# Step sizes by token, sums by triangular matmuls, and a reordered hand-over between two stages of a hybrid block kernel

## The reference, cut to what matters

```python
proj = h @ even_w_in                 # z 512, xbc 1024, dt 8, u 512 columns
z, xbc, dt = split(zxbcdt)
xbc = silu(causal_depthwise_conv(xbc, conv_w, conv_b)); xs, bm, cm = split(xbc)
dt = softplus(dt + dt_bias)          # 512 tokens x 8 heads
a_cs = cumsum(dt * -exp(a_log))      # along the tokens
y = (cm @ bm^T * exp(a_cs[l] - a_cs[s]), causal) @ (xs * dt) + d_skip * xs
y_a = rmsnorm_by_group(y * silu(z)) * norm_gain
y_b = s5_mixer(u)                    # complex-diagonal state space, then a GLU (w_glu)
x = x + concat(y_a, y_b) @ even_w_out
```

## Time and profile before

| | us |
|---|---|
| median of 3 runs | 2755.56 |
| lowest, highest | 2754.64, 2760.26 |
| the profiled execution, device time | 2758.86 |
| its span, first to last instruction | 2757.1 |
| granted TensorE clock, share of full | 0.997 |

### The profile page before, as it was taken

The page is one execution under the profiler, slowest core; times in us unless marked ns, Lnnn a source line. Parts: engine busy times, 40 slices in busy tenths (PEclk is TensorE's granted clock), DMA queues, the critical chain, the costliest instruction groups (busy, mean ns, idle before and its releaser), DMA issues. The chain is left out here.

```text
span 2757.1 us, 33783 instructions
## 1 busy us (share of the span) xinstructions
PE 2704.5 (98%) x12890; PEld 2210.6 (80%) x12890; DVE 1415.8 (51%) x1813; ACT 965.0 (35%) x1350; POOL 223.2 (8%) x212
## 2 busy tenths in 40 slices
PE   8999999899999999999999999999999999999998
PEld 7888877778888888888877888888888787788887
DVE  6676247654443344443486544333898635633334
ACT  5433223543332233332245333222323642422312
POOL 2000014020000000000221000000000000300003
PEclk9999999999999999999999999999999999999999
DMA  4334235232223222232321223333442024222331
GB/s 160 122 134 170 97 116 148 68 122 94 97 99 107 91 89 94 99 107 98 113 69 54 97 93 99 113 107 111 141 135 84 32 70 136 77 99 97 105 105 52
DMA packets 78513, 282.74 MB, mean 103 GB/s; under 512 B 10304, under 2 KB 11456, under 8 KB 77648
## 3 DMA queue, kind: packets, MB, share of 16 engines
q1 hardware_dynamic: 67952, 249.67, 27.2%
q0 software_dynamic: 5856, 25.47, 2.8%
q10 hardware_dynamic: 4608, 6.30, 0.9%
HBM read 261.21 MB, written 13.89 MB: 100 GB/s over the span
## 5 line engine op out<-in xcount | busy, mean ns | idle before, releaser
L201 DVE TENSOR_TENSOR wl<-raw,wh 128x1024 fp32r<-128x1024 f32 (+2 forms) x439 | 564.9, 1287 | 1067.3 <-ACT wh L195 1065.5
L195 ACT ACTIVATE wh<-raw 128x1024 fp32r<-128x1024 f32 (+2 forms) x440 | 480.6, 1092 | 1106.9 <-PE PS L249 919.4
L247 PE MATMUL PS<-Hh,wl 128*128 128x512 f32 x2160 | 846.4, 392 | 9.3 <-DVE wl L201 6.1
L249 PE MATMUL PS<-Hl,wh 128*128 128x512 f32 x2160 | 840.7, 389 | 0.0
L248 PE MATMUL PS<-Hh,wh 128*128 128x512 f32 x2160 | 840.6, 389 | 0.0
L247 PEld LDWEIGHTS PS<-Hh,wl 128*128 128x128 f32 x2160 | 405.5, 188 | 101.0 <-issue 14.9
L248 PEld LDWEIGHTS PS<-Hh,wh 128*128 128x128 f32 x2160 | 405.6, 188 | 85.0 <-issue 1.9
L249 PEld LDWEIGHTS PS<-Hl,wh 128*128 128x128 f32 x2160 | 405.5, 188 | 84.6
L247 PE MATMUL PS<-ffn_gh,wl 128*128 128x512 f32 x880 | 342.7, 389 | 0.0
L249 PE MATMUL PS<-ffn_gl,wh 128*128 128x512 f32 x880 | 342.3, 389 | 0.0
L248 PE MATMUL PS<-ffn_gh,wh 128*128 128x512 f32 x880 | 342.3, 389 | 0.0
(11 more groups left out here) (492 smaller groups left out, 2563.6 us busy)
## 6 DMA issues: line engine op xcount, KB each, us to landing
raw<-in_gu SPq DMA_DIRECT2D x220, 512.0 KB, 3.6
raw<-in_dn SPq DMA_DIRECT2D x80, 704.0 KB, 4.0
raw<-in_hin SPq DMA_DIRECT2D x44, 512.0 KB, 3.6
raw<-in_oin SPq DMA_DIRECT2D x16, 512.0 KB, 3.7
raw<-in_hin_gate SPq DMA_DIRECT2D x16, 512.0 KB, 3.6
X<-QKV ACTq DMA_DIRECT2D x96, 64.0 KB, 2.0
kept_x<-X POOLq DMA_DIRECT2D x16, 256.0 KB, 3.8
raw<-in_eout SPq DMA_DIRECT2D x8, 512.0 KB, 4.0
```

Of the source, the lines that this page charges most:

```text
L195: self.nc.scalar.activation(self.wh[j % SPLIT][:, 0:kw], self.raw[j][:, 0:kw], ACT.Copy).then_inc(self.hi_ready, 1)
L201: self.nc.vector.tensor_sub(self.wl[j % SPLIT][:, 0:kw], self.raw[j][:, 0:kw], self.wh[j % SPLIT][:, 0:kw].bitcast(F32)).then_inc(self.lo_ ...
L247: self.nc.tensor.matmul(out, wl, xh[:, u.k0 + k, :], start=first, stop=False)
L249: done = self.nc.tensor.matmul(out, wh, xl[:, u.k0 + k, :], start=False, stop=last)
```

## The change

- dt becomes part of the u units: a `SideUnit` has ten chunks, eight into its own bank and two into bank 6. The dt stage of four small units is gone.
- `take` scales 8 x 512 once; four matmuls (`turn`) put it by token into 128 x 32, and every later step works on 128 x 32 tiles. The scan gives way to ten matmuls of eight columns with a triangle and ones (`running_sums`). `finish` moves from the second bc unit to the first.
- TOE has a buffer of its own, zeroed by POOL at the start of `even_input` and filled there by POOL's DMAs. `sh_seg` moves into the buffer of Hl.
- The last z unit's read and SiLU, the second split of the GLU weights and the second masking of `CB` move from the end of `even_input` to the start of the joint stage. The 12 products of ones become 2, and 3 and 8 more stand in the first quarter of the joint stage.
- The first two units of the output projection run chunks 4 to 7 in one go each; DVE makes parts 0 and 1 and splits both units ahead of the gates; ACT splits the second unit ahead of a gate.
- `SPLIT_STEP` goes from 6 to 16.
- The table `cols` grows from 310 to 324 columns and the filler `skew` shrinks from 40 to 25, so table and filler together are 349 columns rather than 350.

```diff
 TT = S // P
-SPLIT_STEP = 6
+SPLIT_STEP = 16
+TABLES = 349
...
+class SideUnit(Unit):
+    def __init__(self, kc, side, src, x, bank, side_k0, side_bank, side_start, side_stop):
+        super().__init__(kc + side, src, x, 0, bank)
+        self.main, self.side_k0, self.side_bank = kc, side_k0, side_bank
+        self.side_start, self.side_stop = side_start, side_stop
+    def at(self, k):
+        if k < self.main:
+            return self.bank, k, k == 0, k == self.main - 1
+        return (self.side_bank, self.side_k0 + k - self.main, self.side_start and k == self.main,
+                self.side_stop and k == self.kc - 1)
...
         self.M8 = self.sb("M8", [P, S5G])
-        self.skew = self.sb("skew", [P, 40])
+        self.skew = self.sb("skew", [P, TABLES - dram["cols"].shape[1]])
...
-        v, c0 = self.co.nc.vector, self.co.cols
-        x, e, q, z, z2, rl = self.rows
+        co = self.co
+        self.step(dve, co.nc.vector.tensor_mul(self.ROW, co.PS[0:SSD_H, DT_BANK, :], co.RS[0:SSD_H, :]))
+    def turn(self, pe):
+        co = self.co
+        pe.wait_ge(self.ready, 1)
...
+                                    co.ident[0:SSD_H, 0:SSD_H], start=True, stop=True)
+        m.then_inc(self.turned, 1)
+    def begin(self, dve):
+        v = self.co.nc.vector
+        x, e, q, z, z2, rl, a = self.rows
         k = self.cols["dt_bias"]
-        self.step(dve, v.tensor_mul(x, self.co.PS[0:SSD_H, 4, :], self.co.RS[0:SSD_H, :]))
-        self.step(dve, v.tensor_scalar(x, x, c0[0:SSD_H, k:k + 1], None, ALU.add))
+        bias = self.co.cols[:, k:k + SSD_H].unsqueeze(1).broadcast_to([P, TT, SSD_H])
+        dve.wait_ge(self.turned, 1)
+        self.step(dve, v.tensor_add(self.by_head(x), self.by_head(self.co.PS[:, 7, 0:TT * SSD_H]), bias))
...
         a, k = self.co.nc.scalar, self.cols["a_log"]
-        a.activation(self.W[:, 6, 0:1], self.co.cols[0:SSD_H, k:k + 1], ACT.Exp).then_inc(self.exped, 1)
...
         a.activation(self.rows[1], self.rows[1], ACT.Exp, scale=-1.0).then_inc(self.exped, 1)
+        a.activation(self.A8, self.co.cols[:, k:k + SSD_H], ACT.Exp).then_inc(self.exped, 1)
...
+        x, e, q, z, z2, rl, a = self.rows
...
-        g.memset(self.AT, 0.0).then_inc(self.filled, 1)
...
         v = self.co.nc.vector
-        x, e, q, z, z2, rl = self.rows
+        x, e, q, z, z2, rl, a = self.rows
+        dt = self.AC[:, 32:64]
         dve.wait_ge(self.pooled, 15)
-        self.step(dve, v.scalar_tensor_tensor(self.DT[:], q, 2.0, rl, ALU.mult, ALU.add))
-        self.step(dve, v.tensor_scalar(x, self.DT[:], self.W[:, 6, 0:1], -1.0, ALU.mult, ALU.mult))
-        dve.wait_ge(self.filled, 2)
-        self.step(dve, v.tensor_tensor_scan(self.AT[0:SSD_H, :], self.co.ones8[:], x, 0.0, ALU.mult, ALU.add))
+        dve.wait_ge(self.exped, 2)
+        self.step(dve, v.scalar_tensor_tensor(dt, q, 2.0, rl, ALU.mult, ALU.add))
+        self.step(dve, v.scalar_tensor_tensor(self.by_head(a), self.by_head(dt), -1.0,
+                                              self.A8.unsqueeze(1).broadcast_to([P, TT, SSD_H]), ALU.mult, ALU.mult))
+    def running_sums(self, pe):
+        co, a = self.co, self.rows[6]
+        pe.wait_ge(self.ready, SIZE_STEPS)
+        for t in range(TT):
+            out = co.PS[:, 7, 32 + t * SSD_H:32 + (t + 1) * SSD_H]
+            for k in range(t + 1):
+                m = co.nc.tensor.matmul(out, co.triu if k == t else co.ones[:], a[:, k * SSD_H:(k + 1) * SSD_H],
+                                        start=k == 0, stop=k == t)
+        return m
...
 XBUF = 2
-SIZE_STEPS = 11
+SIZE_STEPS = 10
+DT_BANK = 6
+FILL = (2, 3, 8)
+def cut_products(co, CB, g):
+    d = CB[:, g, 0:S].rearrange("p (t n) -> p t n", n=P)
+    return co.nc.vector.tensor_mul(d, d, co.triu.unsqueeze(1).broadcast_to([P, TT, P]))
...
+    toe_zeroed, toe_in = co.soft_sem("toe_zeroed"), co.soft_sem("toe_in")
+    table = co.dram["s5_k"].rearrange("(m i) n -> i m n", i=16)
...
             def columns():
-                pe.wait_ge(sizes.ready, SIZE_STEPS)
-                for k, src in enumerate((AT[0:SSD_H, :], DT)):
-                    for t in range(TT):
-                        m = nc.tensor.matmul(co.PS[:, 7, (k * TT + t) * 8:(k * TT + t + 1) * 8], src[:, t * P:(t + 1) * P],
-                                             co.ident[0:8, 0:8], start=True, stop=True)
-                m.then_inc(cols_done, 1)
+                sizes.running_sums(pe).then_inc(cols_done, 1)
...
+            def after_x(n):
+                if n == 0:
+                    sizes.turn(pe)
...
             co.multiply(pe, st_u, bank_free)
-            co.multiply(pe, st_dt, dt_bank_free)
-            co.multiply(pe, st_x, bank_free, after=4)
+            co.multiply(pe, st_x, bank_free, after=4, between=after_x)
...
             co.multiply(pe, st_z, bank_free, after=12, between=after_z)
-            pe.wait_ge(z_taken, 1)
-            co.idle_products(0, 12)
+            co.idle_products(0, FILL[0])
...
             d = co.dram["s5_u"]
+            nc.gpsimd.memset(TOE[:, 0:BL - 1, :], 0.0).then_inc(toe_zeroed, 1)
...
             sizes.series(pool)
+            pool.wait_ge(toe_zeroed, 1)
+            for m in range(BL):
+                pool.dma_start(TOE[16 * m:16 * m + 16, BL - 1 - m:BL, :], table[:, 0:m + 1, :]).then_inc(toe_in, 16)
...
             pool.wait_ge(arrived, 16 * len(loads))
-            co.wait_units(pool, st_z, 0, 3)
-            nc.gpsimd.memset(co.Hl[:, 0:BL - 1, :].bitcast(F32), 0.0).then_inc(co.toe_zeroed, 1)
+            pool.wait_ge(toe_in, 16 * BL)
...
             def read_conv(n):
+                if n == 1:
+                    sizes.exponentials(act)
...
                     silu(7)
+                if c == 3:
+                    return
...
             co.run(act, st_u, co.split_hi, lambda i, c: None)
-            co.run(act, st_dt, co.split_hi, lambda i, c: None)
-            co.run(act, st_x, co.split_hi, lambda i, c: read_conv(c), lambda: sizes.exponentials(act))
+            co.run(act, st_x, co.split_hi, lambda i, c: read_conv(c))
             co.run(act, st_bc, co.split_hi, lambda i, c: read_conv(4 + c))
-            co.run(act, st_z, co.split_hi, read_z)
+            co.run(act, st_z, co.split_hi, read_z, late=True)
...
             v = nc.vector
-            dve.sem_inc(dt_bank_free, 1)
...
                 dve.sem_inc(bank_free, 1)
-            def read_dt(i, c):
-                co.wait_units(dve, st_dt, i, c)
-                sizes.take(dve)
+                if c == 3:
+                    sizes.take(dve)
...
                 dve.sem_inc(bank_free, 1)
+                if n == 0:
+                    sizes.begin(dve)
...
                     taps(n - 1)
-                if n == 5:
+                if n == 1:
+                    sizes.quotient(dve)
+                if n == 4:
...
             def read_z(i, c):
+                if c == 3:
+                    return
...
                     take_tokens(3)
-                if c >= 2:
-                    g = c - 2
-                    dve.wait_ge(cb_read, g * TT + TT)
-                    d = CB[:, g, 0:S].rearrange("p (t n) -> p t n", n=P)
-                    v.tensor_mul(d, d, co.triu.unsqueeze(1).broadcast_to([P, TT, P])).then_inc(cut_off, 1)
+                if c == 2:
+                    dve.wait_ge(cb_read, TT)
+                    cut_products(co, CB, 0).then_inc(cut_off, 1)
             co.run(dve, st_u, co.split_lo, read_u)
-            co.run(dve, st_dt, co.split_lo, read_dt)
-            co.run(dve, st_x, co.split_lo, lambda i, c: read_conv(st_x, c, c), lambda: sizes.quotient(dve))
+            co.run(dve, st_x, co.split_lo, lambda i, c: read_conv(st_x, c, c))
             co.run(dve, st_bc, co.split_lo, lambda i, c: read_conv(st_bc, c, 4 + c))
-            co.run(dve, st_z, co.split_lo, read_z, take_columns)
+            co.run(dve, st_z, co.split_lo, read_z, take_columns, late=True)
...
     with ExitStack() as ctx:
-        SEG = co.sb("sh_seg", [P, 3, TRI], ctx=ctx)
+        SEG = co.sb_at("sh_seg", [P, 3, TRI], F32, co.x_end + 4 * DC * S)
...
         T = lambda q: DRIVE[:, 8 * q + 4:8 * q + 8, :].rearrange("p g n -> p (g n)")
-        toe_in = co.soft_sem("sh_toe_in")
+        z_taken, z_active, cut_off = (co.sem(f"sh_{s}") for s in ("z_taken", "z_active", "cut_off"))
...
         def _(sp):
-            table = d["s5_k"].rearrange("(m i) n -> i m n", i=16)
-            sp.wait_ge(co.toe_zeroed, 1)
-            for m in range(BL):
-                sp.dma_start(TOE[16 * m:16 * m + 16, BL - 1 - m:BL, :], table[:, 0:m + 1, :]).then_inc(toe_in, 16)
...
                              d["s5_out"][:, 1024 * q:1024 * q + 1024]).then_inc(arrived[q], 16)
-            sp.wait_ge(toe_in, 16 * BL)
...
                 if q == 0:
-                    pe.wait_ge(toe_in, 16 * BL)
+                    pe.wait_ge(z_taken, 1)
...
                 spread_a(2 * q)
+                if q == 0:
+                    co.idle_products(7, FILL[1])
...
```

(78 more changed lines are left out.)

49 lines of the change are left out of this document (21 added, 28 removed).

## The result

The changed kernel takes 2761.25 us, median of 14 runs (2760.49 to 2766.52); the kernel before took 2757.31 beside it, median of 14 (2753.79 to 2760.26). The ratio is 1.0017, 95% interval 1.0011 to 1.0024: 4 us slower, clear of zero but within the 0.2% or so that the prediction counts as no change, where 16.6 us less was forecast. The profiled execution has a span of 2759.5 us at a granted clock of 0.999.

The account below looks back on a forecast made before the run. PE, busy 98% of the span, was taken as the bound. Gains of 4.7 + 2.9 + 4.5 + 2.4 + 2.1 = 16.6 us took the profiled 2758.86 to 2742.3; less 3.3 to the median, 2739.0, range 2731 to 2748.

Parts of the forecast that it names:

- Table and filler: Stage buffers behind tables and filler: every one moves by 4 bytes, taken as no gain, 2 us either way.
- input stage, stalls less new matmuls: Even mixer's input stage: PE's stalls on DVE's splits shrink, 6.2 us gained, less 1.5 for new column matmuls: 4.7.
- hand-over: From last z unit to first drives on PE: 4.99 us becomes 2.1, gain 2.9, bounds 2.4 to 3.4.
- joint stage: Drives to DVE's second-quarter read: 23.87 us becomes 19.4 with PE at full clock, gain 4.5, bounds 0.9 to 5.
- output begin: Start of the output projection: two PE stalls of about 1.1 us go, gain 2.4, bounds 1.2 to 2.5.
- attention stages: Banded and window attention: the split moved to step 16 lands where ACT and DVE idle, gain 2.1, bounds 1 to 2.3.
- rival (a): PE at half clock from the hand-over into the second quarter; joint gain 0.9 rather than 4.5: 2742.6 us, chance 0.14.
- rivals (a) to (d): Beyond (a), (b): (c) late DMA loads, 2747, chance 0.08; (d) stalls partly stay, 2741.5, 0.05, or all stay, 2751, 0.04.
- rival (b): Joint stage: clock low through all four quarters, 28 us more, 2771 us, slower than before; chance 0.06.

Follow-up runs that it names:

- 348-column version: The changed kernel with its filler one column shorter, so stage buffers begin at byte 118912 as in the kernel before: 2739.50 us, ratio 0.9941 to the kernel before.

## Why the prediction was wrong

The step that failed is "Table and filler": "Every stage buffer moves by 4 bytes. No row shows a price for a position in either direction; I take nothing and 2 us either way." It is wrong twice. The buffers moved by 32 bytes, since the allocator rounds up. And the 2 us had no row behind it: the kernel before holds its large matmuls at one distance modulo 256, so its trace could not show what another one costs, and the edit touches 3408 matmuls on an engine that is busy for 98% of the span. 2 us was 0.6 ns a matmul; it was 6.6, and the term 21.8 us (2761.25 against 2739.50 with only the place put back). A price that nothing bounds, times 3408, should have widened the range upwards and been the rival for the slower side. The purpose of `skew`, a buffer that nothing reads or writes, and of the tables placed between the weight buffers was there to be asked about.

Without this term the sum held against the execution that it was worked out from. Stretches of the traces, before against the 348-column version:

| step | forecast, us less | seen |
|---|---|---|
| input stage, stalls less new matmuls | 4.7 | 6.0 |
| hand-over | 2.9 | 4.1 |
| joint stage | 4.5 | 4.9 |
| output begin | 2.4 | 2.5 |
| attention stages | 2.1 | 1.7 |
| one wait for a split ahead of the window stage | 0 | 1.0 |
| start and end of the span, all else | 0 | -0.8 |
| sum | 16.6 | 19.4 |

The spans say 2757.1 - 2737.7 = 19.4. The medians say less, 2754.62 - 2739.50 = 15.1, and the clock tells why. The kernel before, in the eleven runs beside the 348-column version, took 2753.83 to 2755.03 us in the six with a mean clock of 0.999, 2756.21 and 2757.61 in the two at 0.997, 2759.35 and 2761.61 in the two at 0.995; the profiled one was at 0.997, with the half clock of the joint stage in it. The 348-column version was at 0.999 in all five. Against the six the gain is 14.9 us, which is what the table gives without the joint stage's 4.9 (14.5). So the joint stage's term seems to be worth nothing in one execution and 5 us or more in another; no trace of the kernel before at 0.999 is kept, so this is argued, not shown. Nor does the new kernel hold the clock each time: two of its 14 runs took 2764.72 and 2766.52 at 0.997, the others at most 2762.33.

That 2739.50 is so near to the 2739.0 forecast is therefore in part luck: the sum lacked 2.8 us of gains, and 3.3 us were taken off because the profiled execution lay above the median, although 4.5 of the sum already rested on the half clock in it. The two cancel. Nor do the terms give the range: their best bounds add up to 18.4 us, 20.4 with the 2 for places, which is 2735, not 2731.

**Input stage.** The mechanism was right: the three taps run in 2.31 to 2.36 us throughout, beside POOL too. DVE and then POOL in order of time, of the kernel after:

```profile
433.50 2.36 DVE L1477 SCALAR_TENSOR_TENSOR XC<-XB,cols,XC 128x511 f32<-128x511 f32 x3
437.13 1.23 DVE L222 TENSOR_TENSOR wl<-raw,wh 128x1024 fp32r<-128x1024 f32 x1 [1.27 <-ACT wh L216]
```

```profile
434.49 0.74 POOL L1286 TENSOR_SCALAR SZ<-SZ 128x32 f32<-128x32 f32 x1
...
436.44 0.25 POOL L1287 TENSOR_TENSOR SZ<-SZ 128x32 f32<-128x32 f32 x1
...
437.15 1.32 POOL L1287 TENSOR_TENSOR SZ<-SZ 128x32 f32<-128x32 f32 x1
```

A step on POOL is 0.25 to 0.29 us alone, not 0.44, and up to 1.34 beside a DVE instruction with two inputs. Now the short POOL step is the one that waits, and DVE loses nothing: before, with 1.9 us steps, DVE lost. This agrees with the Trainium skill, "SBUF — State Buffer", section "SBUF: two separate sides": of a DVE instruction with two SBUF inputs and a GpSimd one that reads SBUF, the one that starts first keeps the shared ports for its whole length. The last POOL step above, begun 0.02 us after DVE's split, ends 0.11 us after it. New matmuls cost 2.15 us for the sums and 0.98 for the turning against 1.87 for the old columns, 1.3 rather than 1.5. Some 1 us of the stage's gain I can't attribute.

**Hand-over.** 0.90 us rather than 2.1. The 1.6 us between POOL's last work and PE's start was taken to hold for any meeting; where PE comes last it waited 0.30.

**Joint stage.** 19.0 us from the drives to the second quarter's read, 19.4 forecast. The clock was at 1.00, and the trace without the ones shows it falling; the loss was 2.2 us there, less than the 3.6 of rival (a). None of rivals (a) to (d) occurred in the profiled execution, and rival (b), the only one for the slower side, is not what made the kernel slower.

**Output begin and attention.** As forecast, each confirmed by its own run. The wait of 1.6 us for a split ahead of the window stage became 0.8, with no edit near it. It was 0.8 in most of the runs and 1.5 again in the one without the ones, which does nothing there either; ahead of it DVE waits for a load of X from QKV, 1.78 us before, 1.00 in the 348-column version, 1.82 without the ones. What sets that load's time is open, so the 1.0 us in the table is not counted as the change's worth.

## What to carry to other kernels

Before costing a changed buffer size, write down where every buffer behind it will begin, with the allocator's rounding, and take the distance of each matmul's moving operand to its weights modulo 256 bytes; keep it at zero, in multiples of 32 bytes, in kernels that are bound by float32 matmuls of 512 columns with a weight load between each two, the only kind in which these runs saw the loss. An edit that shifts everything is priced by all that it shifts, not by the lines that it touches: an unknown nanosecond on 3408 matmuls belongs in the range. When one group of untouched instructions shows another mean duration, look at places before looking at the edited stages. And before a term rests on one profiled execution, compare its mean clock with that of the other runs: here the kernel before spans 2753.8 to 2761.6 us, and the clock goes with it.

## What the runs showed of the hardware

With 512 columns of float32 the pace of matmuls, with a weight load between each two, was 226.7 ns where moving operand and weights, in steps of 32 bytes, start at equal places modulo 256 bytes, and 232.8 to 234.2 at the other distances tried (228.9 at +64). It depends on the pair, not on either: moving both by 32 bytes changed nothing (2740.37 us), moving one cost 21.8 us in the changed kernel, some 21 at equal clock in the kernel before (23.7 in the medians) and 46.1 at equal clock when it met the Hh matmuls (47.8 in the medians). Why the distance counts is open; that fetches of the two operands meet somewhere would fit, but no run looks inside. It also stays open why 60 bytes alone is fast, why 384 columns feel nothing, why +64 and -64 differ (228.9 and 233.3), and why an offset of 4 bytes is slow even for both operands together.
